# Interleaving the first two passes of a projection kernel by feature ranges, and moving the first gate sums into later passes

## The reference, cut to what matters

```python
shift, scale, gate = adaln(c, w_ada, b_ada)         # silu(c) @ w_ada (2048 x 6144) + b_ada
h = rms_norm(x, g_norm) * (1.0 + scale) + shift
qa, ka, va, ga, qb, kb, vb, gb = mixer_inputs(h, w_in, q_norm_g, k_norm_g)   # h @ w_in
oa = diff_attention(rope(qa), rope(ka) + cached, va + cached, lam)           # 8 heads, two softmaxes each
ob = gqa_attention(rope(qb), rope(kb) + cached, vb + cached)                 # 8 heads on 2 key/value heads
x = x + gate * mixer_outputs(oa, ob, ga, gb, subln_g, lam_init, w_out)
y = rms_norm(x, g_final)
```

## Time and profile before

| | us |
|---|---|
| median of 3 runs | 1298.14 (1297.83 to 1298.21) |
| the profiled execution's own time | 1300.35 |
| its span, first to last instruction | 1298.5 |
| TensorE busy | 1240.5 (96%) |
| first projection product begins | 44.87 |
| input stage and pass 0, to the end of pass 0 | 44.87 to 142.2 |
| pass 1 | 142.2 to 210.7 |
| pass 2, pass 3 | 81.3 and 80.5 |

### The profile page before, as it was taken

How to read it: one execution, slowest core, us unless ns; L and a number is a source line. 1 busy time by engine, 2 the same in 40 slices (tenths; PEclk the granted TensorE clock), 3 DMA queues, 4 the chain that set the end, 5 groups by cost and what they waited for, 6 DMA issues and landing times.

```text
span 1298.5 us, 17913 instructions
## 1 busy us (share of the span) xinstructions
PE 1240.5 (96%) x6751; PEld 997.1 (77%) x6751; DVE 813.1 (63%) x1295; ACT 601.0 (46%) x1259; POOL 252.1 (19%) x426
## 2 busy tenths in 40 slices
PE   4799988999999999999999999999999999999994
PEld 3455866888888888878787888888787878888883
DVE  4334686748667486565656556565657666769593
ACT  4222314555545546464555555455556655312223
POOL 2010311203011030122212122122223312210102
PEclk9899998999999999999999999999999999999998
DMA  9998452112112131222222221212124423646454
GB/s 336 386 371 288 116 184 65 50 49 86 50 49 71 48 93 49 77 70 74 63 60 79 64 87 50 80 58 79 58 70 138 128 77 104 234 119 248 151 182 179
DMA packets 131094, 156.52 MB, mean 121 GB/s; under 512 B 8144, under 2 KB 98416, under 8 KB 130240
## 3 DMA queue, kind: packets, MB, share of 16 engines
q1 hardware_dynamic: 118032, 111.22, 26.3%
q0 software_dynamic: 12976, 44.15, 10.6%
HBM read 144.18 MB, written 11.16 MB: 120 GB/s over the span
## 4 chain that ended last, share of the span: by engine, by line
PE 85%; DMA 5%; DVE 4%; ACT 2%; POOL 1%; SPq 1%; issue 1%; ACTq 0%; DVEq 0%; POOLq 0%
PE z_ps L605 23%; PE z_ps L607 22%; PE z_ps L606 21%; PE ring L694 5%; PE ring L729 3%; PE ring L794 2%; DMA gate_raw<-in_w_ada_dram 2%; PE ring L800 2%; DMA ada_raw<-in_w_ada_dram 1%; PE ring L627 1%; DVE gate_acc L1439 1%; SPq L571 1%; PE ring L607 1%; PE ring L606 1%; PE ring L803 1%
## 5 line engine op out<-in xcount | busy, mean ns | idle before, releaser
L605 PE MATMUL z_ps<-w_hi,xt_hi 128*128 128x512 f32 x1360 | 562.7, 414 | 7.2 <-DVE xt_lo L1214 3.2
L607 PE MATMUL z_ps<-w_hi,xt_lo 128*128 128x512 f32 x1360 | 533.1, 392 | 0.0
L606 PE MATMUL z_ps<-w_lo,xt_hi 128*128 128x512 f32 x1360 | 531.6, 391 | 0.0
L883 ACT ACTIVATE w_hi<-w_raw 128x512 fp32r<-128x512 f32 x272 | 170.4, 628 | 374.0 <-PE z_ps L607 331.1
L605 PEld LDWEIGHTS z_ps<-w_hi,xt_hi 128*128 128x128 f32 x1360 | 256.3, 188 | 67.8 <-issue 16.4
L607 PEld LDWEIGHTS z_ps<-w_hi,xt_lo 128*128 128x128 f32 x1360 | 255.7, 188 | 56.8
L1220 DVE TENSOR_TENSOR w_lo<-w_raw,w_hi 128x512 fp32r<-128x512 f32 x272 | 194.6, 718 | 155.1 <-ACT w_hi L883 154.8
L606 PEld LDWEIGHTS z_ps<-w_lo,xt_hi 128*128 128x128 f32 x1360 | 257.3, 189 | 39.7
L1297 DVE TENSOR_REDUCE small<-s_sb 128x2 f32<-128x1536 f32 (+1 forms) x60 | 88.3, 1472 | 23.6 <-ACT s_sb L883 22.4
L995 ACT ACTIVATE s_sb<-s_sb,small 128x768 f32<-128x768 f32 (+1 forms) x120 | 97.9, 819 | 1.6 <-DVE small L1297 1.6
L1611 POOL TENSOR_TENSOR sg<-sg,zs 128x128 f32<-128x128 f32 (+1 forms) x60 | 38.3, 638 | 283.2 <-DVE sg L1280 282.5
(11 more groups left out here) (160 smaller groups left out, 1402.2 us busy)
## 6 DMA issues: line engine op xcount, KB each, us to landing
w_raw<-in_w_in_dram SPq DMA_DIRECT2D x192, 256.0 KB, 3.2
ada_raw<-in_w_ada_dram SPq DMA_DIRECT2D x64, 512.0 KB, 10.8
w_raw<-in_w_out_dram SPq DMA_DIRECT2D x64, 256.0 KB, 3.5
gate_raw<-in_w_ada_dram POOLq DMA_DIRECT2D x12, 1024.0 KB, 6.9
o_spill<-row_st POOLq DMA_DIRECT2D x14, 320.0 KB, 3.8
row_st<-o_spill POOLq DMA_DIRECT2D x14, 320.0 KB, 3.4
x_sb<-in_x_sample_dram SPq DMA_DIRECT2D x4, 1024.0 KB, 10.1
w_raw<-in_w_in_dram POOLq DMA_DIRECT2D x16, 256.0 KB, 6.3
```

The costliest lines, as they stand in the source:

```text
L605: pe.matmul(out, hi_l, hi_r, start=start, stop=False)
L606: pe.matmul(out, hi_l, lo_r, start=False, stop=False)
L607: return pe.matmul(out, lo_l, hi_r, start=False, stop=stop)
L883: return act.activation(out, in_, ACT.Copy, **kw)
```

## The change

The five parts:

1. Passes 0 and 1 interleave. `SEGMENTS` cuts each into three ranges of features (0 to 1, 2 to 5, 6 to 15) and alternates them; `ORDER` lists all steps in the new order, and every engine's loop runs over it, with `q` as place in it. As the five `z_ps` banks serve both passes, the sums of a range leave PSUM at its end: ScalarE copies the first ranges into SBUF (`z_part`), VectorE adds later ones (`z_add`), the last into `zs`. Pass 0 keeps its partial sums in `zs`, pass 1 in `part_g`.
2. The 28 modulation pieces after the first block spread over the token tiles of places 0 to 16; a table gives `h` its places.
3. The token transposes use the five `z_ps` banks, and ScalarE's and VectorE's copies lag the squares more. The first two pairs of weights are issued between the norms of the tokens. Eleven pairs instead of eight are issued by GpSimd.
4. The chores at the start of pass 1 (norms, rotary positions of pass 0's keys) follow `chore_step`, six steps later.
5. The first quarter's gate sums leave pass 1. One feature block at a time is loaded (256 KB, one buffer `gate_raw0`) and summed, at steps 2, 10, 13 and 15 of passes 2 to 5. Each next load stands one step behind the sum before it. The products that close the sums move from pass 2 to pass 6.

```diff
-GATE_EARLY = [3, 4, 5, 6, 7, 8, 9, 10]
+GATE_EARLY = [2, 10, 13, 15]
...
+SPLIT_K = 6
+SEGMENTS = [(KV_IT, 0, 2), (G_IT, 0, 2), (KV_IT, 2, SPLIT_K), (G_IT, 2, SPLIT_K), (KV_IT, SPLIT_K, KT), (G_IT, SPLIT_K, KT)]
+SEGMENTS += [(it, 0, KT) for it in range(G_IT + 1, ITS)]
+PARTS = 4
+COPIED, ADDED, LAST_ADDED = (0, 1), (2, 3), (4, 5)
+ORDER = [(it, s) for it, k0, k1 in SEGMENTS for s in range(k0, k1)]
+SEG_OF = [g for g, (it, k0, k1) in enumerate(SEGMENTS) for s in range(k0, k1)]
+EARLY_PAIRS = (SPLIT_K + KT) // 2
...
+def chore_step(it, s):
+
+    return s - SPLIT_K if it == G_IT else s
...
+for _k in range(KT):
+    _it, _s = G_IT + 1 + _k // len(GATE_EARLY), GATE_EARLY[_k % len(GATE_EARLY)]
+    GATE_SUMS[(_it, _s)] = (0, [_k])
+    if _k + 1 < KT:
+        GATE_LOADS[divmod(KT * _it + _s + 1, KT)] = [(0, _k + 1)]
+GATE_LOADS[(G_IT + 1, 1)] = [(0, 0)]
+GATE_SUM_AT[(D_IT + 1, 0)] = GATE_ROWS_AT[(D_IT + 1, 0)] = GATE_OUT_AT[(D_IT + 1, 3)] = 0
...
+def ada_slots(c):
+
+    n = ADA_LOADS[c]
+    if c == 1:
+        return [(3 * e + 1) // 2 for e in range(n)]
+    return [16 + 7 * (ADA_LOAD0[c] - ADA_LOAD0[2] + e) // 2 for e in range(n)]
...
-        take(("HT", i), [1 + i % 2])
+        take(("HT", i), [RING + i % TILES])
...
+            def z_part(g, t):
 
+                act.wait_ge(z_full, TILES * g + t + 1)
+                copy(part_of(SEGMENTS[g][0])[:, t, :], z_ps[:, t, :]).then_inc(z_free, 1)
...
+            def z_add(g, t):
+
+                it = SEGMENTS[g][0]
+                part = part_of(it)[:, t, :]
+                if g in LAST_ADDED and it == G_IT and t == 0:
+                    zs_free(dve, it)
+                dve.wait_ge(z_full, TILES * g + t + 1)
+                dve.tensor_tensor(zs[:, t, :] if g in LAST_ADDED else part, z_ps[:, t, :], part, ALU.add
+                                  ).then_inc(z_free, 1)
...
+                if t in (2, TILES - 1):
+                    load_w(pool, t // 3)
 
-            for j in range(KT // 2):
+            for j in range(2, EARLY_PAIRS):
...
+                c0 = 2 * D_MODEL + NCOL * cc
+                if cc == 0:
+                    if q:
+                        pool.wait_ge(gate_summed, q)
...
+                    pool.dma_start(gate_raw0[:, :], ada_p[:, q, c0:c0 + NCOL]).then_inc(gate0_in, 16)
+                    return
```

More of the change, by code:

```diff
@@ new lines @@
+GATE_LOADS[(G_IT + 1, 1)] = [(0, 0)]
+GATE_SUM_AT[(D_IT + 1, 0)] = GATE_ROWS_AT[(D_IT + 1, 0)] = GATE_OUT_AT[(D_IT + 1, 3)] = 0
+for _cc in range(1, OUTS):
+    _it = OUT_IT + _cc
+    for _i, _s in enumerate(GATE_LATE):
+        GATE_SUMS[(_it, _s)] = (_cc, [2 * _i, 2 * _i + 1])
+    for _q in range(KT // 4):
+        _s = GATE_LATE[2 * (_q - 1) - 1] + 1 if _q >= 2 else 0
+        GATE_LOADS.setdefault((_it, _s), []).append((_cc, _q))
+    GATE_SUM_AT[(_it, 11)] = _cc
+    GATE_ROWS_AT[(_it, 11)] = _cc
+    GATE_OUT_AT[(_it, 12)] = _cc
@@ L195, in count_turns @@
 def count_turns():
-    first, place, used = {}, [], [0] * RING
+    first, place, used = {}, [], [0] * (RING + TILES)
     def take(key, banks):
@@ L331, in build @@
     ident = new("ident", [P, P])
+    gate_sel = new("gate_sel", [P, 2, 2])
     norms = new("norms", [P, 3, DH])
@@ L348, in build @@
         ring = [ctx.enter_context(nc.psum_tensor(f"ring{b}", [P, 512], F32)) for b in range(RING)]
+        banks = ring + [z_ps[:, t, :] for t in range(TILES)]
         def sem(name):
@@ L578, in _ @@
                 load_ada(n)
-            for j in range(KT // 2, ITS * KT // 2):
+            for j in range(EARLY_PAIRS, ITS * KT // 2):
                 load_w(sp, j)
@@ new lines, in _, with between @@
+            for q, (it, s) in enumerate(ORDER[:-W_RING]):
+                pieces = pieces_at(it, s)
+                def between(t):
+                    input_pieces(q, t)
+                    for kind, a, tile, part in pieces[t]:
+                        if kind == "QK":
+                            step_qk(a, part)
+                        elif kind == "S":
+                            step_s(a, tile, part)
+                        elif kind == "T":
+                            step_t(a, tile, part)
+                        elif kind == "V":
+                            step_v(a, tile)
+                        elif kind == "GT":
+                            step_gt(a, tile)
+                        else:
+                            step_o(a, part)
+                project(q, between)
+                if (it, s) in GATE_SUM_AT:
+                    step_gate(GATE_SUM_AT[(it, s)])
```

611 lines of the change are left out of this document (296 added, 315 removed).

## The result

The changed kernel takes 1315.09 us (median of 4 runs, 1314.53 to 1317.95) beside 1298.07 us for the kernel before on the same chip: ratio 1.0131, 95% interval 1.0119 to 1.0143, 1.3% slower. The forecast was 1310.5 us, its range 1299 to 1322. The profiled execution took 1315.53 us, 15.2 more than the one of before. A pass is named by its `it` here: pass 3 is `it` 3.

A forecast was written before the change was run, and what follows sets the result against it. TensorE, busy in 96% of the span, was taken as the bound. From the profiled 1300.35 us, less 24.7 for interleaving, plus 36.9 for the gate sums, gave 1312.6; less 2.2 to the median, 1310.5 was forecast, range 1299 to 1322.

The forecast's parts named there:

- The forecast case: Whole kernel: 24.7 us gained in the first passes, 36.9 lost in passes 2 to 5; 1303 to 1318 us, chance 0.62.
- The wait at step 2: Passes 2 to 5: TensorE idles for the late gate load and the clock falls; 8.6 us in three, 11.1 in pass 2.
- The two sums behind the landing: VectorE, step 2 of passes 2 to 5: two gate sums after the load lands, 1.43 us.
- The other twelve sums at nothing: Steps 10, 13 and 15 of passes 2 to 5: sums lie in VectorE's slack, nothing, at most 1 us a pass.
- The gain of the first two passes: Passes 0 and 1 interleaved (parts 1 to 4): pass 1 ends at 186 instead of 210.7, a gain of 24.7 us.
- the way from there: Second block's end at 60 to pass 1's end: 148 tiles 100.6, 20 modulation pieces 21.2, 4 for the rest; 125.8 us.
- the best case: First two passes: TensorE starts at 38 and never waits, with 2.6 for the low clock; end at 180, gain 31 us.
- The range ends: Five range ends of passes 0 and 1: late copies out of PSUM could delay TensorE; lower end of the gain 15 us.
- The far side: First two passes: range-end copies and adds and late weights eat the interleaving's gain down to 15 or less; 1323 us, chance 0.14.
- The clock that stays up: Passes 2 to 5: waits are paid but the clock does not fall, four times 2.6 less; 1300 us, chance 0.08.
- The quick landing: Step 2 load lands in about 1.6 us, TensorE idles 4.1 us; 21.5 lost against 24.7 gained, 1295 us, chance 0.08.
- No wait at all: Step 2 of passes 2 to 5: VectorE has the sums early and nothing is lost; 1273 us, chance 0.05.

The follow-up runs named there:

- quarter2: Changed kernel with step 2's gate load and sum cut to 128 of 512 columns: 1311.63 us, ratio 1.0113.
- load_first: Changed kernel with the sum left at step 2 but its load issued by GpSimd ahead of the roots of the norms: 1280.00 us, ratio 0.9866.
- sums4: Changed kernel with only 4 of the first quarter's 16 gate blocks loaded and summed, at step 10 of passes 2 to 5: 1280.93 us, ratio 0.9862.
- sum5: Changed kernel with the gate sum of step 2 put at step 5 in passes 2 to 5: 1280.04 us, ratio 0.9868.
- w_late: Changed kernel with sums at steps 5, 10, 13, 15 and the first two weight pairs issued behind all norms, as before: 1279.28 us, ratio 0.9848.
- start_busy: The late-weights kernel (w_late) with 40 idle transposes before the first block's last modulation load and 20 before the first product: 1278.29 us, ratio 0.9842.
- part 5 alone: Kernel before with the first quarter's gate sums moved to steps 5, 10, 13, 15 of passes 2 to 5, nothing interleaved: 1287.84 us, ratio 0.9927.
- after_busy: Changed kernel with 20 idle products of zeros ahead of TensorE's wait for `q_lo` in passes 2 to 5: 1309.98 us, ratio 1.0087.

## Why the prediction was right, and where it was off

**The forecast case.** It came in, with the mechanism of the loss as written and that of the gain in part: 15.2 us more in the profiled execution where I had 12.2, so 3.0 too little. The error is in the gain, 24.7 for 19.6; the loss was 36.9 for 34.8. The other 1.6 of the 4.6 us between forecast and median are the choice of the execution (and 0.1 my rounding): the profiled one of before lay 2.2 us above its median, the one of after 0.4. That the two errors offset each other in part is luck.

**The wait at step 2 (right, 2 us too large).** The path was as written: sum of squares, roots, load, sums, weights, low halves, first score product. Its terms in pass 3: the landing took 3.16 us for the 3.5 of the line between two rows; the idle time 5.5 us for 6.0; the clock 2.8 for 2.6. In pass 2 7.93 for 8.5. The median landing of the 16 loads of 256 KB is on the page:

```profile
gate_raw<-in_w_ada_dram POOLq DMA_DIRECT2D x16, 256.0 KB, 3.2
```

Against the 2.6 us that one works out, as an estimate, from the Trainium skill ("DMA: Bandwidth & Descriptors", "Anatomy of one DMA — SWDGE (gpsimd) path") the trace stands nearer to the 3.5 from the rows: 3.2. For the 64 KB of quarter2 the estimate by that section is 2.15 and the run shows 2.1, so it agrees there.

**The two sums behind the landing** were put at 1.43 us and took 1.74. GpSimd's `sg` operation ran until 300.16, and the first sum, begun at 299.19, took 1.07 of it. load_first, where `sg` is not beside them, has 1.41. The rest of this is in the last section.

**The other twelve sums at nothing (right).** sums4 shows it for those at steps 13 and 15, the passes of sum5 for all.

**The gain of the first two passes (the step that was off, by 5.1 us).** It has two mis-sized terms: the second block ended 1.7 us later than I had, and the way from there took 3.6 us more (0.2 of the two is my rounding).

The beginning: I had 31.5 us for the loads of the first block and 38 for the first projection; they were 35.23 and 42.14. My sum of bytes was short: the windows up to 35.23 hold

```profile
0.00:10.00 10.00, 0.40 (x1) 0.18 (x1) 1.47 (x5) 3.51 (x4) 1.05 (x9) 1.00 0.66 247
10.00:20.00 10.00, 7.40 (x49) 6.92 (x50) 7.57 (x9) 9.41 (x11) 4.83 (x9) 1.00 1.03 401
20.00:30.00 10.00, 5.95 (x96) 4.96 (x96) 6.23 (x9) 4.62 (x10) 4.04 (x6) 0.95 1.08 353
30.00:35.23 5.23, 1.89 (x33) 1.00 (x34) 0.69 (x1) 0.63 (x1) 0.00 (x0) 0.50 1.07 375
```

2.5 + 4.0 + 3.5 + 2.0 = 12.0 MB, not 10.5: loads that the first block doesn't need share the DMA engines with those it does. GpSimd's queue, whose loads of that time are all weights, has 1.57 MB up to 36 us where I had 1:

```profile
q0 software_dynamic: 480, 1.57, 12.2%
```

The rest, about 1 MB, is pieces of the second block, for which the ring of six has room beside the four of the first. Of the 4.1 us, w_late gives back 1.4 (0.9 at least).

The late start moved the second block's end by less than 4.1 us: it is 61.66 for the 60 I had. Here the path was another than the one I wrote. I had the loads bind until 60. In the changed kernel TensorE has no gap from 42.14 to 61.66 (19.52 us busy of 19.52): its own 12 tiles (8.2 us) and 8 pieces (9.6, at the 1.20 read below) fill that time, with 2.0 us for a clock of 0.90 in the mean, low since the waits for the first block and back at about 46. My forecast had no term for that clock; it stands in the best case only. So that the end lies near 60 is in part luck. The loads are close behind, though: in start_busy, which starts at 39.92 with the clock at full, TensorE waits 1.2 us for them in this block, and the block ends at 59.2.

The way from there: 129.4 us for 125.8. A modulation piece between tiles costs more than the 1.06 I had, as my reading stopped at the start of the product behind it, and that product is followed after 0.34 us (61.66 to 62.00) instead of 0.23. From 69.31 to 73.23 with four tiles between, 73.23 to 76.47 with three,

```profile
69.31 1.05 PE L670 MATMUL ring<-ada_raw,cs 128*2 128x256 f32 x16
73.23 1.05 PE L670 MATMUL ring<-ada_raw,cs 128*2 128x256 f32 x16
76.47 1.05 PE L670 MATMUL ring<-ada_raw,cs 128*2 128x256 f32 x16
```

are 3.92 less 2.72 and 3.24 less 2.04, 1.20 each. Twenty of them make 2.8 of the 3.6 us; the rest lies within my choice of 4 for columns and transposes. The range ends, from which I had feared most, cost nothing that shows: TensorE's idle time from 61.66 on is 1.1 us, all before the transpositions of the modulation (`columns`).

What I had not seen is where the gain is from: I had put all of it under the interleaving, while part 5 alone brings 10.3 us of the 18.1 (1298.1 to 1287.8, to 1280.0), or 9.4 of 17.2 beside the kernel before of the same group (1297.25). The stop in pass 1, which my own working priced at 8.4 us, was part 5's to take away.

**The rivals.** The far side (interleaving brings little): the gain lay between it and the forecast. The clock that stays up: it fell in all four waits. The quick landing: quarter2 has one of 2.1 us, and even then the clock fell; my 1.6 us rested on a stop length that the other stops don't bear out. No wait at all: out.

## What to carry to other kernels

Before an operation is put into a busy engine's list, ask not how long it takes but when its operand is issued, and behind what: a sum of 1.4 us at one step cost 34 to 36 us because its load stood in GpSimd's queue behind an operation that waited for VectorE. An issue ahead of that wait, or the sum three steps later, took it all back and turned a change 1.3% slower into one 1.3% faster. Read which stage each part of a change moves: here the smaller-looking edit, taking the sums out of pass 1, brought more (9.4 to 10.3 us) than the interleaving (7.7 to 8.6).

## What the runs showed of the hardware

**VectorE's operations with two inputs in SBUF stood still beside GpSimd's `sg` operation.** In quarter2 an operation of 128 columns took 1.74 us, its twin 0.34. The first ended with GpSimd's `sg` operation (294.42 plus 3.47, less some tenths). In load_first the `w_lo` at 286.63 took 1.91 us, where its neighbours took 0.69, until 288.54; beside it GpSimd's timeline has

```profile
285.00 3.45 POOL L1668 TENSOR_SCALAR sg<-sg 128x1280 f32<-128x1280 f32 x1
```

until 288.45. The kernel before has it too: its `w_lo` at 307.64 took 1.84 us, until 309.48, beside the `sg` of the earlier trace rows, until 309.39. The Trainium skill says so in "SBUF — State Buffer", section "SBUF: two separate sides": such an operation and one of GpSimd that reads SBUF share a pair of ports, whoever comes first has it for the whole instruction, and the other waits. These three cases and the 1.07 us of the changed kernel agree with it: the one that came second ended when GpSimd's did, within 0.3 us.

**The clock has no stop length of its own.** It fell 4.2 us after TensorE's last product (changed kernel), 3.1 (quarter2), and some 1.9 us after the last idle product in pass 2 of after_busy; behind stops of 0.9 us it fell once and stayed up twice. That once it fell 0.9 us after TensorE was back at work and was low for some 3.4 us. In start_busy it fell at 36.0, when TensorE had stood for 1.31 and 1.40 us with a piece of 1.06 us between, and stayed at half until about 39.4, through most of the 20 idle transposes (3.85 us, where 40 of them took 4.59 at the full clock). It came back 5.5 us after work began again in pass 3 of the changed kernel, and 5.2 in the kernel before.
